# Weaving the second layer's front, half by half, between the expert units of a two-layer decoder trunk

## The reference, cut to what matters

```python
for l in range(2):
    if l == 0:
        x = x + even_mixer(rmsnorm(x, ev_norm), ...)
    else:
        x = x + odd_mixer(rmsnorm(x, od_norm), cos, sin, ...)
    x = x + memory_cross_attention(rmsnorm(x, xa_norm[l]), rmsnorm(mem, xa_mem_norm[l]), ...)
    x = x + peer_ffn(rmsnorm(x, ffn_norm[l]), ...)

def odd_mixer(h, cos, sin, ...):
    mq, mk, mv, rx, rg = split(h @ w_in)
    q = apply_rope(rmsnorm(mq, q_norm), cos, sin)
    k = apply_rope(rmsnorm(mk, k_norm), cos, sin)
    c_out = moba_attention(q, k, mv)                  # 8 heads, one block of 256: causal softmax
    d_out = rg_lru(rx, conv_w, ...) * gelu(rg)        # 4-tap causal convolution, linear recurrence over tokens
    return concatenate([c_out, d_out]) @ w_out

def peer_ffn(xn, wq, subkeys, u, v):
    s = einsum(xn @ wq, subkeys)                      # 8 heads, 2 x 128 keys
    eidx, g = top 16 of the pairs of each head        # 8 x 16 = 128 experts for each token
    act = gelu(einsum('td,thkd->thk', xn, u[eidx]))
    return einsum('thk,thkd->td', g * act, v[eidx])
```

## Time and profile before

| | |
|---|---|
| median of 3 runs | 1935.12 us |
| the profiled execution: its own time | 1934.76 us |
| its span, first to last instruction | 1932.9 us |
| mean granted TensorE clock over the span | 0.761 |
| busy: PE, DVE, ACT, POOL | 1454.1, 1011.8, 646.7, 703.2 us |
| moved by DMA | 610.56 MB, of which gathers 536.90 |
| DMA share of the chain that ended last | 39%, PE 35% |

### The profile page before, as it was taken

How to read it: one execution, slowest core, us unless ns; L and a number is a source line. 1 busy time by engine, 2 the same in 40 slices (tenths; PEclk the granted TensorE clock), 3 DMA queues, 4 the chain that set the end, 5 groups by cost and what they waited for, 6 DMA issues and landing times.

```text
span 1932.9 us, 20212 instructions
## 1 busy us (share of the span) xinstructions
PE 1454.1 (75%) x6718; PEld 604.0 (31%) x6718; DVE 1011.8 (52%) x2487; ACT 646.7 (33%) x1897; POOL 703.2 (36%) x516
## 2 busy tenths in 40 slices
PE   7999989556677766777769989985566766667676
PEld 4777778101111111111137766761111111111111
DVE  3332238788544454444441642489974445445444
ACT  1243221423433333333332333123343333333333
POOL 0000001434565655565510000024555555556562
PEclk9999999656666676666669999997766667666666
DMA  8321224999999999999933222359999999999996
GB/s 304 131 88 44 100 110 183 392 415 421 421 421 421 422 421 421 421 421 421 422 147 131 88 88 108 102 233 422 421 421 421 421 422 420 421 422 421 421 421 285
DMA packets 107560, 610.56 MB, mean 316 GB/s; under 512 B 10032, under 2 KB 10176, under 8 KB 41280
## 3 DMA queue, kind: packets, MB, share of 16 engines
q0 software_dynamic: 73728, 536.90, 66.9%
q1 hardware_dynamic: 33728, 72.37, 10.4%
HBM read 608.19 MB, written 1.05 MB: 315 GB/s over the span
## 4 chain that ended last, share of the span: by engine, by line
DMA 39%; PE 35%; DVE 9%; issue 7%; POOL 7%; ACT 4%; POOLq 0%; SPq 0%; ACTq 0%; DVEq 0%; PEldq 0%
DMA arena<-in_experts,idxT 38%; PE psum L518 34%; POOL arena L1718 7%; DVE arena L1424 5%; ACT cst L890 1%; ACT gains L890 1%; ACT arena L890 1%; ACT gelus L890 1%; DVE red L1393 0%; DVE kv L1385 0%; DMA vecs<-in_vecs 0%; ACT sqb L890 0%; DVE rstd L1316 0%; DVE rstd L1304 0%; DVE red L1208 0%
## 5 line engine op out<-in xcount | busy, mean ns | idle before, releaser
L518 PE MATMUL psum<-arena,cst 64*64 64x512 f32 (+1 forms) x4160 | 881.0, 928 | 424.7 <-ACT cst L890 417.6
L1718 POOL DMA_INDIRECT arena<-in_experts,idxT x512 | 703.0, 1373 | 1203.4 <-DVE idxT L1394 579.2
L1424 DVE CUSTOM_DVE_ANT_0 arena<-arena,xrow 128x1024 f32<-128x1024 f32 x512 | 625.0, 1226 | 535.0 <-DMA arena<-in_experts,idxT 533.5
L518 PEld LDWEIGHTS psum<-arena,cst 64*64 64x64 f32 (+1 forms) x4160 | 155.5, 178 | 1144.0 <-ACT cst L890 1099.2
L890 ACT ACTIVATE gelus<-red 128x1 f32<-128x1 f32 x512 | 103.6, 202 | 773.9 <-DVE red L1424 773.6
L518 PE MATMUL psum<-hT,ring 128*128 128x256 f32 x1280 | 295.3, 392 | 6.1 <-DVE hT L1223 6.1
L518 PEld LDWEIGHTS psum<-hT,ring 128*128 128x128 f32 x1280 | 250.4, 197 | 48.5 <-issue 10.3
L890 ACT ACTIVATE cst<-cst,gains 128x128 f32<-128x128 f32 x512 | 206.2, 403 | 16.9
L890 ACT ACTIVATE gains<-gelus,gateT 128x1 f32<-128x1 f32 x512 | 150.7, 294 | 17.0 <-ACT gelus L890 0.2
L890 ACT ACTIVATE arena<-psum 128x512 f32<-128x512 f32 (+3 forms) x89 | 47.8, 544 | 305.5 <-PE psum L518 305.2
L518 PE MATMUL psum<-mixT,ring 128*128 128x256 f32 x256 | 57.5, 388 | 2.0 <-DVE mixT L1697 2.0
(11 more groups left out here) (161 smaller groups left out, 687.2 us busy)
## 6 DMA issues: line engine op xcount, KB each, us to landing
ring<-in_peer_wq SPq DMA_DIRECT2D x8, 2048.0 KB, 7.9
ring<-in_ev_w_in SPq DMA_DIRECT2D x6, 2048.0 KB, 12.4
ring<-in_od_w_in SPq DMA_DIRECT2D x5, 2048.0 KB, 59.2
ring<-in_xa_wkv SPq DMA_DIRECT2D x4, 2048.0 KB, 8.2
arena<-in_experts,idxT POOLq DMA_INDIRECT x512
ring<-in_ev_w_out SPq DMA_DIRECT2D x2, 2048.0 KB, 8.0
ring<-in_xa_wq SPq DMA_DIRECT2D x2, 2048.0 KB, 9.0
ring<-in_xa_wo SPq DMA_DIRECT2D x2, 2048.0 KB, 7.8
```

The costliest lines, as they stand in the source:

```text
L518: return nc.tensor.matmul(out, lhsT, rhs, start=start, stop=stop)
L1424: V.tensor_tensor_reduce(out=ut, in0=ut, in1=xrow[:, u // PAIRS, :], scale=1.0, scalar=0.0, op0=ALU.mult, op1=ALU.add, accum_out=dots[:, k ...
L1718: nc.gpsimd.indirect_dma_start(slot[slot_of(u)], None, d["experts"], bass.IndirectOffsetOnAxis(ap=idxT[:, u:u + 1], axis=0))\
```

## The change

The second layer's front is no longer a stage of its own. It is written as generators, one in each of PE, ACT and DVE. After every expert unit an engine moves its `clock` on and lets its generator run up to the next `until(g)`. The fixed numbers say after which unit a piece is placed:

- memory keys and values of layer 1 from unit 54 (PE: units 64 to 100), in the first layer's half 0;
- `later(0)`, the front of tokens 0 to 127, from unit 128, among the units of the first layer's half 1;
- `later(1)`, the front of tokens 128 to 255, from unit 256, among the units of the second layer's half 0;
- nothing among the last 128 units.

Products in the woven front are 128 columns wide and not 256. All weights of the odd mixer, of `xq`, `xo` and `pq` are loaded twice, once for each half. The norms use TensorE for the sum over features (`column_means`, eight products with `ones`). `ring` keeps three places for weights from `xk1` on, and the fourth holds temporaries (`spare`), so `arena` stays with the slots. The sub-keys of layer 1 go into halves of `hT` and `mixT`. POOL goes from layer 0 to layer 1 with no stop but the `idx_ready` of each 32 units. PSUM banks are now named by kind: the sums of a half and their transposes take two, the woven front turns through four others.

```diff
+MEMORY_FROM = 54
+LATER_FROM = (PAIRS, 2 * PAIRS)
+LATER_RING = 3
+FRONT_BANKS = 4
...
+    values(1)
+    for t in range(TT):
+        for n in ("rx", "mq", "mk", "mv", "rg"):
+            out.append((f"od_{n}{t}", cols(d["od_w_in"], OD[n]), f"{n}.{t}"))
+        out += [(f"od_out{t}{b}", cols(d["od_w_out"], 512 * b), f"od_out{t}.{b}") for b in range(2)]
+        rest(1, f"1{t}", f"1{t}")
...
+            def experts(l, t, fronts, previous=None):
...
+                    clock[0] = l * UNITS + u + 1
+                    next(fronts, None)
...
+            def later(t):
+                g = LATER_FROM[t]
...
+                yield from until(g + 9)
+                column_means("od", t)
+                yield from features4(f"rx.{t}", f"od_rx{t}", 512, 0, hh, KC, beats(11), (3 * t,))
+                yield from features4(f"mq.{t}", f"od_mq{t}", 512, 0, hh, KC, beats(15))
...
+                yield from features4(f"mk.{t}", f"od_mk{t}", 512, 0, hh, KC, beats(19), between={2: gates})
...
+                yield from features4(f"rg.{t}", f"od_rg{t}", 512, 0, hh, KC, beats(32))
...
+                for b in range(2):
+                    yield from features4(f"od_out{t}.{b}", f"od_out{t}{b}", 512, 0, mixh, KC, beats(44 + 4 * b))
...
+                yield from features4(f"xq1{t}", f"xq1{t}", 512, 0, hh, KC, beats(55), (3 * t + 1,))
...
+                for q in range(4):
+                    yield from features4(f"pq1{t}.{q}", f"pq1{t}{q}", 512, 0, hh, KC, beats(77 + 4 * q),
...
+                for n in range(18):
+                    yield from until(g + 84 + 2 * n)
+                    route_late(1, t, n)
...
-            norm("od")
-            for b, n in enumerate(("mq", "mk")):
...
-            cross(1)
-            peer(1)
...
-                    if u == PAIRS:
-                        pool.wait_ge(idx_ready, 8 * l + 8)
```

More of the change, by code:

```diff
@@ L875, in _ @@
-            peer(1)
-            assert seen[0] == len(JOB)
+            ahead = fronts()
+            previous = None
+            for l in range(LAYERS):
+                for t in range(TT):
+                    experts(l, t, ahead, previous)
+                    previous = (l, t)
+            clock[0] = LAYERS * UNITS
+            for _ in ahead:
+                pass
+            back(*previous)
+            assert sum(opened) == len(JOB)
         @block.scalar
@@ L881, in _, with until @@
             count = [0]
+            clock = [0]
+            def until(g):
+                while clock[0] <= g:
+                    yield
             def link(ins):
@@ L1021, in _, with fronts @@
+            def fronts():
+                yield from until(MEMORY_FROM)
+                yield from memory_keys()
+                for t in range(TT):
+                    yield from later(t)
             load_table(EXP_LN_SET)
@@ L1182, in _ @@
+            for _ in ahead:
+                pass
+            rows_out(*closed[-1], closed[-2])
         @block.vector
@@ L1434, in peer, with add_back @@
+            def add_back(l, t):
+                for b in range(2):
+                    o = full(dve, f"back{l}.{t}.{b}")
+                    xs = xT[:, 4 * b:4 * b + 4, t * P:(t + 1) * P]
+                    V.tensor_tensor(xs, xs, o.rearrange("p (c n) -> p c n", n=P), ALU.add)\
+                        .then_inc(bank_free(f"back{l}.{t}.{b}"), 1)
+            def peer(fronts):
+                norm("ffn0", xT, vec("ffn_norm0"), hT, h_ready)
                 for g in range(4):
-                    best_keys(0, 4 * g, 4)
+                    best_keys(0, 0, 4 * g, 4)
@@ L1706, in _ @@
+            clock[0] = LAYERS * UNITS
+            for _ in ahead:
+                pass
+            add_back(*closed[-1])
+            copied(dve, "back1.1.0", "back1.1.1")
         @block.gpsimd
```

1330 lines of the change are left out of this document (833 added, 497 removed).

## The result

The changed kernel took **1782.18 us**, the median of 4 runs between 1781.14 and 1782.63. Before stood at 1935.3 beside it. The ratio is 0.9206, with a 95% interval of 0.9190 to 0.9222: faster by 153 us. The forecast was 1811, in a range of 1765 to 1890. The profiled execution took 1781.85 us for a span of 1779.4, so 2.5 us lie outside the span (before: 1.9).

What follows compares the result with a forecast made beforehand. DMA was taken to bound the gather stages, with its queues nearly empty in the fronts. 1932.9 - 283.3 - 10.6 + 135 = 1774.0 us, plus 35 for waits and 1.9 outside the span, gave 1811 us, range 1765 to 1890.

Steps and rivals of the forecast that it cites:

- The hole: Front of layer 1, between the layers' gathers: the time lost to the DMA queues goes, -283.3 us.
- the restart: Remaining 249 gathers of layer 1: 630.6 us against 620.0 at full pace, so -10.6 us.
- The loads: Woven stages: 25 weight blocks newly load under gathers at 5.4 us each, +135 us.
- The pace of 3.26 us a unit: Units 14 to 88 of a woven half: gathers slowed by loads, 10.5 blocks x 23.0 = 241.5 us.
- the share of loads: DMA in woven halves: loads take no larger share than a quarter, else the prediction is wrong.
- TensorE 239 us: Units 9 to 94 of a woven half: TensorE's work at clock 0.95 fits within 269 us of DMA.
- Ten exchanges at 4.3 us: Each woven half: about ten waits between engines, 43 us, bounds 0 to 8.6 us for one.
- The waits add 35 us: Woven halves: TensorE with waits exceeds DMA by 13 and 18 us, plus 4 for unevenness; bounds 0 and 117.
- Engines' waits bind: Rival, woven halves: each exchange costs up to 8.6 us, giving 1893 us; chance 0.15.
- Weights late: Rival, woven halves: the last block in each half comes 23.0 us late, giving 1857 us; chance 0.05.
- Slow clock: Rival, units 9 to 94 of woven halves: TensorE's clock below 0.74 means slower than before, 2007 us at 0.66; chance 0.05.
- POOL shut out: Rival, gather issues: POOL loses VectorE's work in the old front, at most 107 us, giving 1918 us; chance 0.03.

Runs made afterwards that it cites:

- thin: The changed kernel with each weight load from block xk1 on cut to an eighth of its bytes (a quarter for xo): 1740.8 us, ratio 0.900.
- few: The changed kernel with all loads, but the woven projections do only half of their products: 1779.51 us.
- lag: The changed kernel with ScalarE's and VectorE's woven pieces one unit later (the shift), TensorE's unchanged: 1780.52 us, ratio 0.9208.
- slots6: The changed kernel with six slots for gathers in place of eight: 1806.59 us.
- packed: The changed kernel with woven weights laid out as one contiguous 16 KB piece per partition, not eight of 2 KB: 1772.30 us.
- fewpacked: The changed kernel with woven weights in contiguous 16 KB pieces and half of the woven projections' products left out: 1766.09 us.
- beforeloads: The kernel before the change with one weight block loaded 16 times more under the first layer's gathers: 2023.15 us against 1934.74, ratio 1.0457.
- lagpacked: The changed kernel with ScalarE's and VectorE's woven pieces one unit later and woven weights in contiguous 16 KB pieces: 1766.89 us, ratio 0.9135.
- lagthin: The changed kernel with ScalarE's and VectorE's woven pieces one unit later and an eighth of the load bytes: 1688.47 us.

## Why the prediction was right, and where 29 us went

**The hole, -283.3, and the restart, -10.6: right.** The second layer follows at 2.48 us, and the 127 steps from unit 384 to 511 take 318.0 us, 320.5 for a whole half at that pace (forecast 319).

**The loads, 25 x 5.4 = +135: right.** The price measures 5.5 by itself; 25 x 5.53 would be 138. In the halves the same price can be read off. Against 320.5 for a half without loads, the first woven half is 74.4 us longer and the second 60.3. The hardware queue's lines for them are:

```profile
q1 hardware_dynamic: 13296, 28.31, 18.8%
```

```profile
q1 hardware_dynamic: 10176, 22.02, 15.2%
```

That is 13.5 and 10.5 blocks, so 5.5 and 5.7 us a block, all waits included. The other five blocks load in the first layer's half 0, where four did before. The first half carries three of the next one's, as the prediction said of units 216 to 256. That makes the halves 395 and 381 and not 400 each.

**The pace of 3.26 us a unit from unit 14 to 88, 241.5 us: right,** 241.3 and 241.8. So is the share of loads, below a quarter in the first stretch: 21.29 of 99.34 MB. (From 760 to 860 us alone it is 10.64 of 41.26, 26%.)

**TensorE 239 us, and 244 in the second half: right within 4%.** Its busy time from unit 137 to 222 and from 265 to 350 is 233.1 and 235.0 us. The clock was lower than the 0.95 taken, 0.91 and 0.92. A product 128 wide took 0.265 us (1184 records, two to a product, of 156.9 us) and was costed at 0.2525 / 0.95 = 0.266. The forms of the changed kernel:

```profile
L578 PE MATMUL psum<-hT,ring 128*128 128x128 f32 x1184 | 156.9, 288 | 2.8 <-DMA ring<-in_peer_wq 2.8
L578 PE MATMUL psum<-mixT,ring 128*128 128x128 f32 x288 | 37.3, 281 | 0.0
```

The two fronts of the changed kernel as windows:

```profile
695.67:972.42 276.75, 233.10 (x1631) 135.88 (x1624) 151.24 (x341) 129.66 (x350) 98.03 (x85) 0.91 1.02 412
1090.24:1367.68 277.44, 235.01 (x1655) 137.35 (x1649) 153.62 (x339) 131.58 (x350) 96.80 (x85) 0.92 1.02 410
```

**Ten exchanges at 4.3 us, 43 us a half: not refuted.** In `thin` TensorE is idle 39.1 and 40.8 us, which is an upper bound, since ordinary waits of the units are among it; the shift takes 13 to 14 away. What one exchange costs was not measured by itself.

**"The waits add 35 us": this step failed.** It took the excess of the engines' side over DMA's, 282 and 287 us against 269, so 13 and 18 us, and 4 for unevenness. Measured are 271.4 and 275.7 in `thin` against 274.2 and 272.8 for DMA in `few`: an excess of nothing and 3. The 16 us between 13 and -3 in the first half are 7 for TensorE's work (232.3 and not 239), 4 for its idle time (39.1 and not 43) and 5 for DMA (274.2 and not 269); in the second half 9, 2 and 4. Each term was right within some 10%, but their small difference was not. That both sides came out so nearly equal was not foreseen. What is left can be read from the runs: `few`, in which TensorE can't bind, is 2.7 us faster, and `lag` 1.7, which is below what the runs can tell. So waits add about 3 us. The sum is then 1774.0 + 3 for the dearer load + 3 = 1780, and the span is 1779.4. The lower bound of that term, 0, was the nearer one. That a wait beside a full DMA isn't added to its time was in the prediction, and `lag` bears it out; how many slots that takes, `slots6` doesn't settle. The range's upper end, 1890, was also to take in the waits' bound of 1893, and falls 3 us short of it.

**The rivals.** *Engines' waits bind:* no, but only just; in `packed` the engines' side does in the second half, for 6 us. *Weights late:* TensorE's idle for `ring` is 2.4 and 2.8 us in the whole kernel. *Slow clock:* 0.91 in the stretch; a clock near 0.74 stood in no woven stretch of any run (the lowest is 0.86, in `fewpacked`), so what it would cost was not tried. *POOL shut out:* an issue took less than before, though VectorE's woven pieces now stand among the gathers:

```profile
L2144 POOL DMA_INDIRECT arena<-in_experts,idxT x512 | 628.3, 1227 | 1125.1 <-PE psum L578 744.6
```

The mean is 1227 ns in place of 1373, and DMA is full, at a share of 1.02 in both woven stretches. An issue that starts within VectorE's expert product is still the longer one, 1.45 us in the mean against 0.94 in the first woven stretch. Nothing of it shows in the bandwidth: `fewpacked`, where VectorE does the same work, moves 421 GB/s there. Why such an issue takes longer was not shown.

## What to carry to other kernels

When a stage that leaves DMA idle is woven into one that fills it, count the bytes it brings under the transfers, at a price measured in a window with both queues busy; that gave nearly the whole answer here. Waits between engines then cost only what the time of their side exceeds DMA's by, plus what the buffers can't hide (`lag` took 32 us of ScalarE's waits away in the first woven half and gained 1.7 us), so compute both sides first, and remember that cutting one of two equal sides shows nothing until both are cut. An excess that is a small difference of two large sums is less sure than either, so give it a wide bound. Once the sides are equal, shorten both: here larger pieces for the loads gave 10 us by themselves, and the consumers' pieces one step behind the producer's, worth nothing alone, gave another 5 on top.

## What the runs showed of the hardware that was not expected

- With weight loads in 2 KB pieces the rate of all that moves together was lower: 412 GB/s in the woven stretch (414 in `lag`) and 415 in `beforeloads`, against 420 and 421 with 16 KB pieces in `fewpacked` (417 in `packed`, 422 in `lagpacked`). Large pieces were worth 10 to 14 us of 1780.
- TensorE's granted clock was lower where its expert units came further apart, and high where other products filled the gaps: 0.65 with a unit each 2.5 us (the last half), 0.54 with one each 3.1 us and nothing between (`beforeloads`), 0.91 with the woven projections between them. It rose to 0.97 in the second half of `lagthin`, where TensorE was busy 220.88 of 248.10 us, 89%.
- POOL's issue of a gather got shorter in the woven stretches. An issue that starts within VectorE's expert product is long. Counted from the timelines, from 500 to 980 us before, 115 of 190 start so and take 1.84 us in the mean, the others 0.94; in the first woven stretch it is 33 of 75, at 1.45, and the others still 0.94. In the last half, 68 of 121 and 1.83 are as before. Why fewer fall there and those are shorter was not tried further.
